# Expert rows of the second half of the tokens in engine loops of one unit (16 rows), with 16 slots from row 128 on

## The reference, cut to what matters

```python
def peer_ffn(xn, wq, sub_keys, u_tab, v_tab):
    ...
    q = jnp.matmul(xt, wq).astype(jnp.float32).reshape(t, PEER_HEADS, 2, PEER_SUBDIM)
    scores = jnp.einsum('thcd,hcnd->thcn', q, sub_keys.astype(jnp.float32))
    sv, si = lax.top_k(scores, PEER_TOPK)
    cand_s = (sv[:, :, 0, :, None] + sv[:, :, 1, None, :]).reshape(t, PEER_HEADS, PEER_TOPK * PEER_TOPK)
    ...
    best_s, best_p = lax.top_k(cand_s, PEER_TOPK)
    idx = jnp.take_along_axis(cand_i, best_p, axis=-1)
    gate = jax.nn.softmax(best_s, axis=-1)
    ...
        act = jnp.einsum('td,thkd->thk', xb.astype(jnp.float32), u_tab[ib].astype(jnp.float32))
        wgt = jax.nn.gelu(act) * gb
        return jnp.einsum('thk,thkd->td', wgt, v_tab[ib].astype(jnp.float32))
```

## Time and profile before

| | |
|---|---|
| time, median of 3 runs | 2317.18 us (2313.78 to 2320.38) |
| span of the profiled execution | 2316.7 us; its page gives no other time for it, and the three runs lie within 3.7 us of it |
| busy: PE, DVE, ACT, POOL | 88%, 74%, 36%, 29% |
| rows 0 to 255 of layer 0, first dot product to last | 843.1 us to 1495.5 us |
| rows 0 to 255 of layer 1, first dot product to last | 1655.4 us to 2304.5 us |
| gathers | 512 of 1 MB, 536.90 MB of the 700.42 MB moved |
| instruction queues | q8 47 packets, 0.77 MB; q14 64 packets, 0.52 MB |

### The profile page before, as it was taken

One profiled execution on the slowest core, in us unless ns is written; L12 is line 12 of the kernel. 1 busy time (PEld: TensorE's weight loads), 2 busy tenths in 40 slices (PEclk: granted clock), 3 DMA queues, 4 the chain that ended last, 5 costly groups with the idle time before them and its releaser, 6 DMA issues. The chain is left out here.

```text
span 2316.7 us, 28383 instructions
## 1 busy us (share of the span) xinstructions
PE 2045.0 (88%) x8624; PEld 1313.5 (57%) x8624; DVE 1719.1 (74%) x4183; ACT 845.3 (36%) x2058; POOL 667.6 (29%) x627
## 2 busy tenths in 40 slices
PE   8999999999989899998778778798999987787776
PEld 6779987779979665544323233296655443333232
DVE  6757776667777577778787787575787787877875
ACT  6656655666657641212111111176312121111110
POOL 1300002200001033444444444110244445445441
PEclk9999999999999999999999998999999999999999
DMA  6255433354526569999999999765699999999996
GB/s 226 99 188 190 180 104 122 119 183 175 182 97 188 207 238 407 412 421 421 421 422 421 421 422 422 307 195 208 233 415 410 421 421 421 421 422 422 422 421 267
DMA packets 138663, 700.42 MB, mean 302 GB/s; under 512 B 14392, under 2 KB 40248, under 8 KB 66872
## 3 DMA queue, kind: packets, MB, share of 16 engines
q0 software_dynamic: 73728, 536.90, 56.1%
q1 hardware_dynamic: 64824, 162.22, 20.1%
HBM read 698.03 MB, written 1.05 MB: 302 GB/s over the span
## 5 line engine op out<-in xcount | busy, mean ns | idle before, releaser
L2111 PE MATMUL bank<-ARENA 128*128 128x512 f32 x2048 | 983.1, 628 | 203.6 <-PEq L2109 201.3
L2111 PEld LDWEIGHTS bank<-ARENA 128*128 128x128 f32 x2048 | 389.4, 199 | 776.4 <-issue 775.6
L2006 POOL DMA_INDIRECT ARENA<-in_uv_rows,ARENA x512 | 570.7, 1115 | 741.0 <-PE bank L2111 642.9
L2427 DVE CUSTOM_DVE_ANT_0 ARENA<-ARENA 128x1024 f32<-128x1024 f32 x512 | 625.2, 1221 | 208.2 <-DMA ARENA<-in_uv_rows,ARENA 200.1
L157 PE MATMUL bank<-PARTS,PARTS 128*128 128x256 f32 (+6 forms) x1488 | 469.7, 316 | 0.0
L2234 ACT ACTIVATE ARENA<-ARENA 128x1 f32<-128x1 f32 x512 | 103.3, 203 | 1003.7 <-DVE ARENA L2427 1003.3
L158 PE MATMUL bank<-PARTS,PARTS 128*128 128x256 f32 (+6 forms) x1488 | 469.4, 315 | 0.0
L156 PE MATMUL bank<-PARTS,PARTS 128*128 128x256 f32 (+3 forms) x1424 | 459.2, 322 | 6.6 <-DVE PARTS L561 2.8
L157 PEld LDWEIGHTS bank<-PARTS,PARTS 128*128 128x128 f32 (+2 forms) x1488 | 285.1, 192 | 13.6 <-issue 1.0
L158 PEld LDWEIGHTS bank<-PARTS,PARTS 128*128 128x128 f32 (+2 forms) x1488 | 284.5, 191 | 14.0
L156 PEld LDWEIGHTS bank<-PARTS,PARTS 128*128 128x128 f32 x1424 | 273.1, 192 | 24.9 <-issue 4.4
(11 more groups left out here) (275 smaller groups left out, 1930.9 us busy)
## 6 DMA issues: line engine op xcount, KB each, us to landing
ARENA<-in_w_up_tiles SPq DMA_DIRECT2D x44, 1024.0 KB, 6.3
ARENA<-in_w_down SPq DMA_DIRECT2D x44, 512.0 KB, 3.6
ARENA<-in_w_out SPq DMA_DIRECT2D x32, 512.0 KB, 4.5
ARENA<-in_wq_tiles SPq DMA_DIRECT2D x16, 1024.0 KB, 13.6
ARENA<-in_w_in SPq DMA_DIRECT2D x40, 384.0 KB, 4.0
ARENA<-in_w_in SPq DMA_DIRECT2D x24, 512.0 KB, 8.7
ARENA<-in_w_in SPq DMA_DIRECT2D x40, 256.0 KB, 3.2
ARENA<-in_uv_rows,ARENA POOLq DMA_INDIRECT x512, 22.4
```

The source lines that it names most:

```text
L2006: nc.gpsimd.indirect_dma_start(out=slot[slot_of[i]], out_offset=None, in_=table[:, :], in_offset=bass.IndirectOffsetOnAxis(ap=picked[:, t, ...
L2111: last = mm(row_banks[t][n][:, :], diag[i % N_DIAG], slot[slot_of[i]][:, D + n * 512:D + (n + 1) * 512], start=(c == 0), stop=(c == NPICK ...
L2427: v.tensor_tensor_reduce(u, u, xn[:, t, :], 1.0, 0.0, ALU.mult, ALU.add, dots[:, t, c:c + 1]).then_inc(S("dots_ready"), 1)
```

## The change

Rows 128 to 255 no longer stand written out on VectorE, ScalarE and GpSimd. VectorE and ScalarE run the first six of the eight late units in a loop of one unit and have the last two written out. GpSimd has rows 128 to 143 written out, then a loop of two units with three turns, then the last unit. TensorE's loop is now one of 16 rows and six turns, from row 144. To make the turns alike, row r of every late unit has its own slot (`late_home[r]`), so that there are 16 slots from row 128 on, four of them new (where query weights lay before); the diagonals have 16 places instead of four; dots, gelus and gates of a unit lie in fixed places; VectorE hands the numbers of the next unit over in a fixed place (`picked_next`), which GpSimd copies before it uses them; ScalarE copies the scores of the unit to be chosen to a fixed place (`scores_now`). GpSimd waits for VectorE's numbers on `late_numbers` and for a free slot on `slot_free`, which it counts down itself. The exponential of the gate stands behind row 4 of a unit instead of row 1. `add_out(0)`, the addition of the first half's sum to X, stands ahead of the last unit instead of behind row 132.

```diff
-        row_loaded = [nc.alloc_semaphore(f"row_loaded{s}") for s in range(SLOTS)]
+        row_loaded = [nc.alloc_semaphore(f"row_loaded{s}") for s in range(16)]
...
+            SLOTS_AT += [WQ_AT + s * 2 * D for s in range(4)]
             slot = [arena(at, 2 * D) for at in SLOTS_AT]
+            late_home = [12, 13, 14, 15, 6, 7, 8, 9, 10, 11, 0, 1, 2, 3, 4, 5]
...
-            slot_of = [i % FEW if i < N_FEW else (i - N_FEW) % SLOTS for i in range(len(rows))]
+            LATE = NPICK
+            slot_of = [i % FEW if i < N_FEW else (i - N_FEW) % SLOTS if i < LATE else late_home[i % TOPK]
+                       for i in range(len(rows))]
...
-                        sp.wait_ge(S("row_used"), 250)
+                        sp.wait_ge(S("row_used"), LATE + 10)
                         next_loads(sp, 0, PIECES // 2)
...
-                    for i, (t, c) in enumerate(rows):
+                    for i, (t, c) in enumerate(rows[:LATE + TOPK]):
...
+                    def late_rows(unit):
+                        now = picked_now[unit % 2]
+                        pool.wait_ge(S("late_numbers"), 1)
+                        pool.sem_inc(S("late_numbers"), -1)
+                        nc.gpsimd.tensor_copy(now, picked_next)
+                        pool.drain()
+                        for r in range(TOPK):
+                            pool.wait_ge(S("slot_free"), 1)
+                            pool.sem_inc(S("slot_free"), -1)
+                            nc.gpsimd.indirect_dma_start(
+                                out=slot[late_home[r]], out_offset=None, in_=table[:, :],
+                                in_offset=bass.IndirectOffsetOnAxis(ap=now[:, r:r + 1], axis=0)
+                            ).then_inc(row_loaded[late_home[r]], 16)
+
+                    with pool.Fori(0, (len(units) - first_late - 2) // 2):
+                        late_rows(first_late + 1)
+                        late_rows(first_late + 2)
+                    late_rows(len(units) - 1)
...
-                        last.then_inc(S("row_used"), 1)
+                        last.then_inc(S("slot_free") if LATE <= i < len(rows) - TOPK else S("row_used"), 1)
...
-                            for i in range(i0, i0 + SLOTS):
+                            for i in range(i0, i0 + TOPK):
                                 add_row(i)
 
-                    looped = [(132, 10)]
+                    looped = [(LATE + TOPK, len(units) - first_late - 2)]
...
+                    def late_gelus(done, args=None, scores=None):
+                        for r in range(TOPK):
+                            act.wait_ge(S("dots_ready"), done + (r + 1))
+                            nc.scalar.activation(late_gelu[:, r:r + 1], late_dots[:, r:r + 1], ACT.Gelu_apprx_tanh
+                                                 ).then_inc(S("late_gelu"), 1)
+                            if r == 4 and args is not None:
+                                act.wait_ge(S("gate_arg"), args)
+                                nc.scalar.activation(gate_raw, gate_raw, ACT.Exp,
+                                                     accum_out=gate_sum[:, first_late:first_late + 1]).then_inc(S("gate_exp"), 1)
+                            if r == 9 and scores is not None:
+                                nc.scalar.copy(scores_now, scores).then_inc(S("scores_now"), 1)
...
+                    with act.Fori(0, n_late - 2) as it:
+                        late_gelus(it * TOPK + LATE, it + (first_late + 2), late_sc[:, it, :, 1, :])
+                    late_gelus(LATE + TOPK * (n_late - 2), len(units))
+                    late_gelus(LATE + TOPK * (n_late - 1))
...
+                    def late_unit(turn, choose=True, numbered=True):
+
+                        w = choices[1]
+                        for r in range(TOPK):
+                            u = slot[late_home[r]][:, 0:D]
+                            dve.wait_ge(row_loaded[late_home[r]], turn * 16 + loaded_by(LATE + r))
+                            v.tensor_tensor_reduce(u, u, xn[:, 1, :], 1.0, 0.0, ALU.mult, ALU.add, late_dots[:, r:r + 1]
+                                                   ).then_inc(S("dots_ready"), 1)
+                            if r == 0:
+                                dve.wait_ge(S("gate_exp"), turn + (first_late + 1))
...
+                            else:
+                                late_diagonal(r - 1)
+                            if r == 3 and numbered:
+                                gate_args(w, gate_raw)
+                                numbers_of(w, picked_next, done="late_numbers")
+                            if r == 11 and choose:
+                                dve.wait_ge(S("scores_now"), 1)
+                                dve.sem_inc(S("scores_now"), -1)
+                                first_choice_of(w, [scores_now[:, side, :] for side in range(2)])
+                            if r == 15 and choose:
+                                best_eight_of(w)
+                                next_eight_of(w)
+                        late_diagonal(TOPK - 1)
+                        dve.sem_inc(S("late_gelu"), -TOPK)
+
+                    def late_diagonal(r):
+                        dve.wait_ge(S("late_gelu"), r + 1)
+                        v.tensor_scalar(late_diag[r], ident, late_gelu[:, r:r + 1], gate_now[:, r:r + 1],
+                                        ALU.mult, ALU.mult).then_inc(S("diagonals_waiting"), 1)
...
-                    for i in range(len(rows)):
+                    for i in range(LATE):
...
-                    diagonal(len(rows) - 1)
+                    diagonal(LATE - 1)
+                    dve.wait_ge(S("sc_taken"), len(steps))
+                    with dve.Fori(0, n_late - 2) as it:
+                        late_unit(it)
+                    late_unit(n_late - 2, choose=False)
+                    add_out(0)
+                    late_unit(n_late - 1, choose=False, numbered=False)
                     add_out(NT - 1)
```

More of the change, by code:

```diff
@@ L1713, in second_layers @@
             diag = [arena(diag_at + i * P, P) for i in range(N_DIAG)]
+            late_diag = [arena(HT_AT + r * P, P) for r in range(TOPK)]
+            late_dots, late_gelu = dots[:, 1, 0:TOPK], gelu_dots[:, 1, 0:TOPK]
+            gate_raw, gate_now = gate[:, 1, 0:TOPK], gate[:, 1, TOPK:2 * TOPK]
+            picked_next = picked[:, 1, TOPK:2 * TOPK]
+            picked_now = [picked[:, 1, (2 + p) * TOPK:(3 + p) * TOPK] for p in range(2)]
             def choice(at, eq_at):
@@ L1730, in second_layers @@
             gate_sum = arena(gate_sum_at, len(units))
+            late_sc = shaped(Q_AT + 4 * T + 4 * NKEY, 6, 2, NT, NKEY)
+            scores_now = shaped(HT_AT + TOPK * P, 2, NKEY)
+            first_late = LATE // TOPK
+            n_late = len(units) - first_late
             steps = ([(h, (0,)) for h in range(3)] + [(3, (0, 1))] + [(h, (1,)) for h in range(3)]
@@ L2148, in rows_in_a_loop @@
                         with nc.tensor.Fori(0, count):
-                            for i in range(i0, i0 + SLOTS):
+                            for i in range(i0, i0 + TOPK):
                                 add_row(i)
-                    looped = [(132, 10)]
-                    inside = [i for i0, count in looped for i in range(i0, i0 + count * SLOTS)]
+                    looped = [(LATE + TOPK, len(units) - first_late - 2)]
+                    inside = [i for i0, count in looped for i in range(i0, i0 + count * TOPK)]
                     for i in range(len(rows)):
@@ L2347, in first_choice, with first_choice_of @@
                         t, h = units[u]
-                        w = choices[u >= AHEAD]
                         dve.wait_ge(S("sc_taken"), step_of[t, h] + 1)
+                        first_choice_of(choices[u >= AHEAD], [sc[h][:, side, t, :] for side in range(2)])
+                    def first_choice_of(w, scores):
                         for side in range(2):
-                            v.max(w.sv[:, side, 0:8], sc[h][:, side, t, :])
+                            v.max(w.sv[:, side, 0:8], scores[side])
                         dve.drain()
                         for side in range(2):
-                            v.max_index(w.siu[:, side, 0:8], w.sv[:, side, 0:8], sc[h][:, side, t, :])
-                            v.match_replace(w.rest[:, side, :], w.sv[:, side, 0:8], sc[h][:, side, t, :], -3e38)
+                            v.max_index(w.siu[:, side, 0:8], w.sv[:, side, 0:8], scores[side])
+                            v.match_replace(w.rest[:, side, :], w.sv[:, side, 0:8], scores[side], -3e38)
                         dve.drain()
@@ L2366, in best_eight, with best_eight_of @@
                     def best_eight(u):
-                        w = choices[u >= AHEAD]
+                        best_eight_of(choices[u >= AHEAD])
+                    def best_eight_of(w):
                         v.max(w.bv[:, 0:8], w.best)
@@ L2390, in numbers, with numbers_of @@
                         t, h = units[u]
```

(6 more changed lines are left out.)

26 lines of the change are left out of this document (17 added, 9 removed).

## The result

The changed kernel takes 2385.14 us (median of 5 runs, 2377.95 to 2390.76), the kernel before 2314.82 us (5 runs, 2313.78 to 2320.38): a ratio of 1.0295, 95% interval 1.0276 to 1.0315. It is 70 us slower; I had forecast 10 us faster. The profiled execution has a span of 2377.6 us.

What follows compares the result with a forecast made beforehand. Transfers bound the second half (421 GB/s), with one late DMA engine setting the end. Saved fetches of 9.7 us, all else nothing, took the profiled 2316.7 to 2307.0, so 2307.5 us by median; range 2303.5 to 2317.5.

Steps and rivals of the forecast that it cites:

- GpSimd's new wait: At each late unit GpSimd waits for VectorE's numbers and copies them; hidden by an 11 us margin, cost 0.
- Rival 3: At each late unit, numbers over 11 us later make GpSimd starve the DMA engines: 2321 us, chance 0.04.
- The late DMA engine and the fetches: Second half: one DMA engine lags; five of seven code fetches saved a layer, 0.97 us each, 9.7 us in all.
- The lateness at the end: End of each second half: from fall of DMA share to last dot product, 7 us instead of 12.
- Jumping back fetches nothing: VectorE's late loop: its jumps back cause no code fetches, so two fetches are left of seven a layer.
- rival 2: VectorE's late loop fetches again at each jump: two a turn 2330.8 us, chance 0.06; one 2319.1, chance 0.05.
- 16 slots: Second half's gathers: 12 slots already cover a gather's 22.6 us, so four more gain nothing.
- Smaller things: ScalarE's score copy, loop register operations, PE's longer loop and the moved add_out(0): hidden or as before, priced at nothing.

Runs made afterwards that it cites:

- experiment 1: Changed kernel with GpSimd's drain behind its copy of the numbers replaced by a semaphore it waits for: 2304.91 us, ratio 0.996 to the kernel before.
- Experiment 5: Changed kernel with the semaphore for the drain and VectorE's six looped units written out again: 2312.16 us, ratio 0.9989 to the kernel before.
- Experiment 3: Changed kernel with the semaphore for the drain and at most 12 gathers in flight instead of 16: 2304.43 us, ratio 0.9955 to the kernel before.
- experiment 4: Kernel before with one GpSimd drain in each layer, ahead of the second half's fifth unit: 2330.26 us, ratio 1.0063.

## Why the prediction was wrong

**The step that failed** is *GpSimd's new wait*, "Counted and hidden: 0". It took the wait for VectorE's numbers and the copy, and left out the instruction between the copy and the sixteen gathers, the drain, which stands in the diff. Its price by the runs: 7 drains in each layer, 5.5 us each, 77 us. The mechanism in one line: GpSimd's drain waits for the landing of the gathers that GpSimd has started, a gather into the empty queue is used 5.6 us after its start (1250.71 to 1256.31), and whatever is bound by transfers loses that time at each drain.

Could it have been seen in the trace of before? Only with care. That kernel has drains on GpSimd, for instance between these two operations:
```profile
1566.90 0.20 POOL L1594 TENSOR_SCALAR STAT<-STAT 128x8 f32<-128x8 f32 x1 [27.81 <-DVE STAT L1553]
1567.25 1.79 POOL L1596 TENSOR_TENSOR STAT<-STAT,HALF 128x8 f32<-128x8 f32 x1
```
From the end of the first to the start of the second there are 0.15 us, drain included, though the DMA engines are busy just then:
```profile
1566.90:1567.50 0.60, 0.60 (x5) 0.60 (x5) 0.53 (x2) 0.58 (x2) 0.45 (x2) 1.00 0.73 229
```
Those are SyncE's transfers. So the row tells two things: this drain was nearly free on an engine with no transfer of its own in flight, and it didn't wait for those of another queue. It does not tell what a drain costs with gathers in flight. No drain of the kernel before stands in the stretch in which gathers are in flight, so its price had to be bounded from above, by the time that a gather needs to land, 22.6 us for each of 14. It would have stood as a rival with a price; I never priced it at all.

The Trainium skill, Perfetto Trace Analysis, section Sequencer-only Instruction (DRAIN, etc), lists a drain as an instruction of the sequencer with a semaphore wait and an execution of its own, and names no transfers that it would wait for; that agrees with the 0.15 us above and not with the 23.5 us behind gathers. The Trainium skill, Perfetto Trace Analysis, section DMA Instruction — SWDGE (GPSIMD), says that a gather's end in the profile is the end of descriptor generation and not of the data movement; this trace agrees (0.94 us in the row, 5 us and more to the landing). This is the reason why "GpSimd has finished its gathers" can't be read from its busy rows.

**Rival 3** had the place and the look of it ("gathers landing in bursts", a DMA share under 1) but another cause (late numbers) and 2321 us. That figure is also too low by its own rule: 14 us on top of 2307.5 is 2321.5, which lies within the 7 us of 2317.2 that the prediction calls no change. Its cause exists and costs nothing: in experiment 1, which keeps the wait, the numbers hold GpSimd up 14 times, by at most 7.0 us:
```profile
POOL ARENA L2032 <- POOLq L2031: 86.3, 14, 7.0
```
and transfers go on at 422 GB/s. The range, up to 2317.5, left out both.

**The steps that held**, once the drain was out of the way:
- *The late DMA engine and the fetches.* Predicted: five fetches of seven saved in each layer, 9.7 us. Measured by lengths: 5.2 and 5.0 us; by medians 11.4 (2316.32 to 2304.91), about 6 to 12 by the interval. From row 127 to row 255 of layer 1 the prediction had said some 320 us; in experiment 1 it is 320.0 (1967.16 to 2287.1). These are its rows 127 (L2492, still written out) and 128, and 242 and 243:
```profile
1967.16 1.22 DVE L2492 CUSTOM_DVE_ANT_0 ARENA<-ARENA 128x1024 f32<-128x1024 f32 x1 [0.78 <-DMA ARENA<-in_uv_rows,ARENA]
...
1971.64 1.22 DVE L2511 CUSTOM_DVE_ANT_0 ARENA<-ARENA 128x1024 f32<-128x1024 f32 x1
...
2253.90 1.23 DVE L2511 CUSTOM_DVE_ANT_0 ARENA<-ARENA 128x1024 f32<-128x1024 f32 x1 [0.99 <-DMA ARENA<-in_uv_rows,ARENA]
...
2257.34 1.22 DVE L2511 CUSTOM_DVE_ANT_0 ARENA<-ARENA 128x1024 f32<-128x1024 f32 x1 [1.95 <-DMA ARENA<-in_uv_rows,ARENA]
```
128 even steps would take 318.1 us, so 1.9 are left: two broken steps, one between rows 139 and 142, the other from row 242 to 243 (3.44 us). Seven and two, as predicted. The length from row 128 on would have said five and none, but row 128 (no wait in its line) starts some 2 us later than its gather would have let it, in both kernels. Experiment 5 brings four of the five back; what the fifth belongs to was not tried.
- *The lateness at the end.* Predicted 7 us instead of 12. In experiment 1 the DMA share falls like this before the last row is used at 2287.1:
```profile
2275.00:2280.00 5.00, 3.94 (x9) 1.38 (x9) 3.01 (x7) 0.41 (x2) 0.00 (x0) 1.00 0.98 410
2280.00:2285.00 5.00, 3.94 (x9) 1.35 (x8) 3.04 (x7) 0.41 (x2) 0.00 (x0) 1.00 0.21 84
```
Fifteen engines are through at about 2281, so the last one is 6 us behind.
- *Jumping back fetches nothing* (against rival 2). In experiment 1 two packets came on q14 in layer 1 while VectorE's loop ran its six turns (1971.6 to 2210 us), where two for each turn would be twelve. The step that breaks between rows 139 and 142 lies in the first turn, and no later turn has one. The Trainium skill, Runtime: NRT & Kernel Launch, Instruction fetch mechanics, has a taken branch fetch its target if that lies outside a window of two pages; this loop of 79 rows of code stays quiet, which agrees with the reading that its first block is still there.
- *16 slots: nothing.* Experiment 3. *Smaller things: nothing.* Their sum lies within what experiment 1 leaves between 9.7 and 11.4 us.

In the changed kernel itself the saved fetches (3 packets in layer 1's second half as well) brought nothing visible beside the loss, since each drain puts the sixteen engines back in step and so takes the lateness away that the fetches cause (read from the rate rows above and from rows 207 to 211 of experiment 4; no run was made for it alone). That is also how it comes to 4.6 and 5.0 us for a drain against the kernel before (32.0 / 7, 34.7 / 7) and 5.3 and 5.7 against experiment 1.

## What to carry to other kernels

Price every added instruction that can wait, drains and fences above all, with what its engine has in flight at that place, not with what the same instruction cost where nothing was in flight. To order a small operation before a gather on GpSimd, give the operation a semaphore and wait for that: it cost 0.90 us here in place of 23.5. When the transfers are the bound and their share falls under 1, look for the one place in a period where the queue runs empty; then ask which instruction stands there in the program, and trust that more than the name of the releaser.

## What was unexpected of the hardware

- GpSimd's drain waited for the landing of gathers it had started. GpSimd stood for 23.5 to 27.0 us with 16 slots, 19.2 to 23.3 with 12, 10.5 and 11.5 at row 32 with 10, and for 0.15 us with no gather in flight while SyncE's transfers ran.
- Behind a drain no DMA engine lags, by the rate rows; in the kernel before, one ends a second half 12 us behind, and each fetch of VectorE's code is 0.97 to 0.98 us of that. Two fetches of ScalarE's and GpSimd's code added nothing.
- A single drain cost 7.4 and 6.3 us where the late engine was some 7 us behind, 4.6 and 4.9 us in the first half.
